# FFN start: second unit's fifth and sixth product ahead of the first unit's seventh, and GpSimd's sums for them released earlier

## The reference

```python
    u2 = _rmsnorm(h, ln2_g[i])
    a, bb = jnp.split(u2 @ w_gate_upffn[i], 2, axis=-1)
    h = h + (jax.nn.silu(a) * bb) @ w_down[i]
```

## Time and profile before

| what | value |
|---|---|
| time of the program, median of 3 | 1633.21 us (1632.21 to 1633.38) |
| time of the profiled execution | 1631.67 us |
| its span | 1629.7 us |
| TensorE busy (matmul) | 1605.5 us, 99% |
| VectorE busy | 1148.1 us, 70% |
| first product of unit 0 / of unit 2 starts | 458.06 / 499.22 us |
| VectorE busy in the 22.2 us from 457.80 to 480.00 | 22.13 us |
| VectorE busy in the 20 us from 480 to 500 | 19.16 us |
| TensorE busy in the 100 us from 600 to 700 | 100.00 us |

### The profile page before, as it was taken

One profiled execution on the slowest core, in us unless ns is written; L12 is line 12 of the kernel. 1 busy time (PEld: TensorE's weight loads), 2 busy tenths in 40 slices (PEclk: granted clock), 3 DMA queues, 4 the chain that ended last, 5 costly groups with the idle time before them and its releaser, 6 DMA issues.

```text
span 1629.7 us, 21081 instructions
## 1 busy us (share of the span) xinstructions
PE 1605.5 (99%) x7644; PEld 1307.3 (80%) x7644; DVE 1148.1 (70%) x1650; ACT 629.0 (39%) x1012; POOL 709.5 (44%) x390
## 2 busy tenths in 40 slices
PE   9999999999999999999999999999999999999997
PEld 5888888888877888888888788887878888877775
DVE  6342788863499777777776766886986995399557
ACT  6221444421165444444444222254562012268214
POOL 2435111155514333322226688671555554544552
PEclk9999999999999999999999999999999999999999
DMA  5511110141514443334449995323201111110012
GB/s 199 87 56 39 40 38 28 33 152 61 219 73 157 158 150 148 143 146 165 154 158 353 404 393 232 143 78 116 65 27 39 50 41 52 39 53 27 14 39 104
DMA packets 54566, 190.31 MB, mean 117 GB/s; under 512 B 5857, under 2 KB 7842, under 8 KB 53834
## 3 DMA queue, kind: packets, MB, share of 16 engines
q1 hardware_dynamic: 49362, 171.66, 29.0%
q10 hardware_dynamic: 5112, 17.44, 3.6%
HBM read 134.02 MB, written 55.05 MB: 116 GB/s over the span
## 4 chain that ended last, share of the span: by engine, by line
PE 84%; DVE 8%; issue 3%; DMA 2%; ACT 2%; POOL 1%; SPq 0%; DVEq 0%; ACTq 0%; POOLq 0%
PE G L832 37%; PE U L1102 11%; PE G L1102 10%; PE U L1140 6%; PE G L1140 6%; PE G L1176 4%; PE U L996 1%; DMA hid_spill<-hst 1%; PE U L1384 1%; DMA raw<-in_weights 1%; PE G L1373 1%; DVE ring_lo L2424 1%; DVE X_lo L2419 1%; DVE h L2529 1%; PE U L877 1%
## 5 line engine op out<-in xcount | busy, mean ns | idle before, releaser
L633 POOL TENSOR_SCALAR w_hi<-raw 128x1024 fp32r<-128x1024 f32 x48 | 143.0, 2979 | 274.0 <-PE G L832 213.4
L832 PE MATMUL G<-B_hi,w_hi 128*128 128x512 f32 x480 | 149.5, 393 | 0.2 <-ACT yb L1942 0.2
L832 PE MATMUL G<-B_lo,w_hi 128*128 128x512 f32 x480 | 148.0, 390 | 0.0
L832 PE MATMUL G<-B_hi,w_lo 128*128 128x512 f32 x480 | 147.9, 389 | 0.0
L832 PE MATMUL G<-A_hi,w_hi 128*128 128x512 f32 x432 | 138.4, 402 | 0.0
L677 POOL TENSOR_TENSOR S<-fraw 128x512 f32<-128x512 f32 x33 | 46.9, 1422 | 202.7 <-DVE ring_lo L2424 194.5
L832 PE MATMUL G<-A_lo,w_hi 128*128 128x512 f32 x432 | 133.6, 390 | 0.0
L832 PE MATMUL G<-A_hi,w_lo 128*128 128x512 f32 x432 | 133.3, 390 | 0.0
L635 POOL TENSOR_TENSOR w_lo<-raw,w_hi 128x1024 fp32r<-128x1024 f32 x48 | 127.6, 2658 | 4.0
L1667 ACT ACTIVATE ring_hi<-S 128x512 fp32r<-128x512 f32 x132 | 82.0, 628 | 111.8 <-PE U L1140 34.0
L1102 PE MATMUL G<-X_hi,ring_hi 128*128 128x512 f32 x308 | 120.1, 390 | 2.3 <-DVE sf L2439 1.2
(11 more groups left out here) (440 smaller groups left out, 3815.9 us busy)
## 6 DMA issues: line engine op xcount, KB each, us to landing
raw<-in_weights SPq DMA_DIRECT2D x72, 512.0 KB, 3.6
hid_spill<-hst SPq DMA_DIRECT2D x72, 512.0 KB, 2.6
fraw<-in_weights SPq DMA_DIRECT2D x66, 512.0 KB, 4.5
Dc<-hid_spill SPq DMA_DIRECT2D x56, 512.0 KB, 12.7
Dc<-hid_spill ACTq DMA_DIRECT2D x14, 512.0 KB, 7.9
h<-in_x_t SPq DMA_DIRECT2D x8, 512.0 KB, 7.8
h_spill<-h SPq DMA_DIRECT2D x8, 512.0 KB, 6.8
pj_spill<-pj_out SPq DMA_DIRECT2D x8, 512.0 KB, 3.6
```

What stands on the lines that cost most here:

```text
L633: pool.tensor_scalar(hi, raw[:, u, :], 1.0, None, ALU.mult).then_inc(w_hi_done, 1)
L832: mm = pe.matmul(G[g][:, b * HT:(b + 1) * HT], w, x[:, k, b * HT:(b + 1) * HT], start=s0, stop=s1)
```

## The change

Three things are changed, all in units 0 and 1 of the FFN. TensorE takes a new list `START` for its first 14 products, in which (1, 4) and (1, 5) stand ahead of (0, 6). The two special waits of GpSimd's sums for unit 1 are gone: S2 now waits for `weights_lo(0, 4)` and S4 for `weights_lo(0, 5)`, as in all other units. ScalarE's and VectorE's written orders are turned accordingly: on ScalarE `take(0, 4)` moves behind `weights_hi(1, 4)`, and `weights_hi(1, 6)` behind `weights_hi(2, 1)`. On VectorE `quarter(0, 1)` moves ahead of `operand_lo(5)`, then come `weights_lo(1, 4)`, `quarter(0, 3)`, `weights_lo(1, 5)`, and only then `weights_lo(0, 6)` and `operand_lo(6)`. The last pair of units keeps the old list.

```diff
+START = [(0, 0), (0, 1), (1, 0), (1, 1), (0, 2), (0, 3), (1, 2), (1, 3), (0, 4), (0, 5), (1, 4), (1, 5), (0, 6), (1, 6)]
 FIRST = [(0, 0), (0, 1), (1, 0), (1, 1), (0, 2), (0, 3), (1, 2), (1, 3), (0, 4), (0, 5), (0, 6), (1, 4), (1, 5), (1, 6)]
...
                 def free(r):
 
-                    if w == 1 and r == 5:
-                        pool.wait_ge(x_lo, 2 * NR)
-                    elif w == 1 and r == 4:
-                        pool.wait_ge(f_lo[0], turn(0, NR - 1))
-                    elif w:
+                    if w:
                         pool.wait_ge(f_lo[(w - 1) % 2], turn(w - 1, r))
...
-            for w, r in FIRST:
+            for w, r in START:
                 product(w, r)
...
-            take(0, 2), take(0, 4), take(1, 0), take(1, 2)
-            weights_hi(1, 4), weights_hi(1, 5), weights_hi(1, 6)
-            weights_hi(2, 0), weights_hi(2, 1)
+            take(0, 2), take(1, 0), take(1, 2)
+            weights_hi(1, 4), take(0, 4), weights_hi(1, 5)
+            weights_hi(2, 0), weights_hi(2, 1), weights_hi(1, 6)
             take(1, 4), silu(0)
...
-            weights_lo(0, 5), operand_lo(5)
-            weights_lo(0, 6), quarter(0, 1), quarter(0, 3), operand_lo(6)
-            weights_lo(1, 4), quarter(1, 1), quarter(1, 3), quarter(0, 4), weights_lo(1, 5)
-            quarter(0, 5), weights_lo(1, 6), quarter(0, 6), weights_lo(2, 0), weights_lo(2, 1)
+            weights_lo(0, 5), quarter(0, 1), operand_lo(5)
+            weights_lo(1, 4), quarter(0, 3), weights_lo(1, 5), weights_lo(0, 6), operand_lo(6)
+            quarter(0, 4), quarter(1, 1), quarter(1, 3), quarter(0, 5)
+            weights_lo(1, 6), quarter(0, 6), weights_lo(2, 0), weights_lo(2, 1)
             quarter(1, 4), weights_lo(2, 2), weights_lo(2, 3), gated_quarter(1, 1), gated_quarter(1, 4)
```

## The result

The changed kernel is slower: 1636.48 us median (1634.37 to 1638.92, 13 runs) against 1632.33 us for the kernel before (1630.94 to 1633.38, 11 runs), timed beside it. The ratio is 1.0025, 95% interval 1.0017 to 1.0032. The difference of the medians is 4.15 us; 4.1 was forecast. The profiled execution took 1634.37 us, the fastest of the 13 runs.

A forecast was written before the change was run, and what follows sets the result against it. TensorE is busy 1605.5 of 1629.7 us, and the time of `quarter(0,6)` was taken to set (2,6). Adding 3.5 + 0.55 = 4.1 us to the 1633.21 median gave 1637.3, range 1634.0 to 1639.0 (8 in 10).

The forecast's parts named there:

- Part 3: (0,6) directly ahead of (1,6) in ring slot 6: refill exposed, TensorE waits 1.6 us, `quarter(0,6)` 3.5 us later.
- Part 2: New order up to (1,4): after `operand_lo(5)` and `weights_lo(1,4)`, product (1,4) starts at 489.0.
- Part 1: Unit 1's freed GpSimd sums collide with VectorE at `operand_lo(4)`, 1.10 us, and `operand_lo(5)`, 0.8: 1.9 us.
- the prediction's own sign: On VectorE: the prediction is wrong if VectorE isn't held up near 480.6 and 485.2.
- The last term: At `weights_lo(1,6)`: a collision with GpSimd's unit 2 sums costs 0 to 1.10 us, half taken, 0.55.
- the sum 3.5 + 0.55: `quarter(0,6)` 3.5 us later plus 0.55 for a collision at `weights_lo(1,6)`: 4.1 us in all.
- The reading of what carries everything: The time of `quarter(0,6)` sets the start of (2,6), by a fixed chain of 21.65 us.
- (B): GpSimd's freed sums don't hold VectorE up, 1.9 us not paid: +1.6 to +2.7, no measurable change; chance 0.24.
- (C): Full block at `weights_lo(1,6)` and one more between 500 and 520: +5.7 us, 1638.9; chance 0.12.
- (D): (1,4) follows (0,5) at once, short refill at (1,6), up to 1.87 us back: 1631.3; chance 0.07.
- No new wait behind: After (2,6), expected near 521 in place of 516.87, no new wait was to appear.
- Part 4's spare time: On ScalarE: `weights_hi(1,6)` behind `weights_hi(2,0)` and `(2,1)`, whose load lands by 495.65, has 0.6 us to spare.

The follow-up runs named there:

- e3: Changed kernel with (0,6) between (1,4) and (1,5), ScalarE's and VectorE's orders turned to fit; ratio to before 1.0011, `operand_lo(4)` to unit 3 40.93 us.
- e5: Kernel before with only GpSimd's two special waits removed, no order touched; ratio to before 1.0000, `operand_lo(4)` to unit 3 39.14 us.
- e8: Changed kernel with `quarter(0,3)` directly behind `quarter(0,1)`, ahead of `operand_lo(5)`; one run, `operand_lo(4)` to unit 3 43.15 us against 42.86.
- e2: Changed kernel with unit 1's S2 and S4 over 8 of 512 columns, the rest left out; ratio to before 1.0010, `operand_lo(4)` to unit 3 41.13 us.
- e4: Kernel before with `quarter(0,6)` ahead of `weights_lo(1,6)` on VectorE; timed three times, ratios to before 0.9994, 0.9993 and 0.9994.
- e1: Changed kernel with `quarter(0,6)` ahead of `weights_lo(1,6)` on VectorE; ratio to before 1.0020, `operand_lo(4)` to unit 3 41.92 us.
- e7: Changed kernel with the edits of e2 and e3 at once; ratio to before 1.0000, `operand_lo(4)` to unit 3 39.13 us.
- e9: Rebuilt kernel: TensorE's and ScalarE's orders as in e3, VectorE's quarters and refills reordered; ratio to before 1.0000, `operand_lo(4)` to unit 3 39.29 us.
- e6: Changed kernel with `weights_lo(0,4)` ahead of `weights_lo(1,3)` on VectorE; one run, `operand_lo(4)` to unit 3 42.78 us against 42.86.

## Why the prediction was right

**The side, the size and most of the path were right.** Slower by over 0.2% was forecast with 0.62; the ratio is 1.0025 with the lower end of its interval, 1.0017, just under that bound, so slower is clear of the interval and over 0.2% only likely. The median, 1636.48, lies 0.8 below the forecast and in the range. That 0.8 comes from the starting point, a median of three runs (1633.21) that lay 0.9 above the 1632.33 of the eleven; the difference itself is 4.15 where 4.1 was forecast, closer than the interval (2.8 to 5.2 us) can tell.

**Part 3, the slot, was right.** Forecast: (0,6) over at 497.3, (1,6) at 498.9 plus up to 1.1, a new wait of 1.6 to 2.7. Measured: 497.01, 498.97, and 1.80. e3 takes 1.93 of the 3.66 away by putting one product between the two users.

**Part 2 was right**: (1,4) was forecast at 489.0 and came at 488.71.

**Part 1 came out near in its sum and wrong in its step.** The step "GpSimd then gets its turn, and `operand_lo(4)` waits 1.10" failed: GpSimd was kept out for 4.9 us and `operand_lo(4)` was not touched. By the prediction's own sign, VectorE held up near 480.6 and 485.2, half of it failed: there was no delay at 480.6, and no wait of (0,4) for `X_lo`. Both sums then fell on `operand_lo(5)`, 1.59 in place of the 1.9 reckoned for the two places. That the sum nearly held is luck in part, since e5 shows the same freed sums costing nothing where quarters happen to lie right, and e8 S4 kept out altogether. That collisions of this kind are on the path is shown by e2: 1.73, with the smaller one at `weights_lo(1,6)` in it.

**The last term was 0.37, not 0.55**: `weights_lo(1,6)` lasted 1.05 in place of 0.68. In the prediction's terms the sum 3.5 + 0.55 came out as 3.25 + 0.37 = 3.62 at `quarter(0,6)`, the 3.25 being smaller by the 0.3 that Part 1 had reckoned too much.

**The reading of what carries everything held for the change, and was stated too strongly.** From `quarter(0,6)` to (2,6) it is 21.65 before, 21.66 in the changed kernel, and 21.69 in e4. But it is 22.36 in e1, 22.61 in e7, 22.84 in e3 and 23.42 in e9. The chain isn't fixed: it is the longest of several of nearly one length, and where the quarter is pulled ahead in a new product order, ScalarE's queue (e3, e7, e9) or VectorE's with its collisions with unit 2's sums (e1, e9) takes over. It foretells what a delay costs better than what an advance brings.

**Rivals.** (B), no collision on the path, is refuted by e2; its remark that GpSimd might be let in later did come true, but the sums then fell on `operand_lo(5)` and were paid all the same. (C), two more full blocks, didn't come. (D), all hidden, didn't come: (1,4) did follow (0,5) at once, but (0,5) had itself waited 1.49, and the refill ahead of (1,6) was not short.

**No new wait behind** was forecast; there is one of 0.45 ahead of (2,5), which costs nothing at (2,6).

**Part 4's spare time** for `weights_hi(1,6)` behind unit 2's tiles was put at 0.6; it was 0.17, and e8 shows what happens when it is gone.

**What stays open.** Unit 3 starts 3.66 late, but the span is only 2.7 longer. TensorE's timelines of the down products, the first matmul of all, in the changed kernel and before, and the only one with a wait in the next 20 us, before:

```profile
885.76 0.61 PE L1137 MATMUL G<-Dc,ring_hi 128*128 128x512 f32 x2
```

```profile
882.15 0.62 PE L1140 MATMUL G<-Dc,ring_hi 128*128 128x512 f32 x2
...
901.99 0.70 PE L1140 MATMUL G<-Dc,ring_hi 128*128 128x512 f32 x2 [0.64 <-DVE h L2529]
```

Up to the start of the down products the delay is carried almost whole: 3.61. Most of what is given back is the wait of 0.64 at 901.99 for VectorE's `h`, which the trace of the changed kernel doesn't have. This wait takes one of three sizes in the 14 traces: none (changed, e5, e6), about 0.6 (before and seven others, the three of e4's kernel among them), and 1.8 (e1, e7, e9). So one pair of spans is a poor measure of the change. The medians, 4.15 apart, don't show the 0.8 given back. Whether the size of this wait belongs to a kernel or to an execution was not tested.

## What to carry to other kernels

When two products share a ring slot, the gap between them must cover the way TensorE, ScalarE, VectorE and back: here 1.96 us from the end of (0,6) to the start of (1,6), and it also delays whatever stands behind the refill in those two queues. Before freeing an engine that shares a port with a saturated one, look at which instructions it will fall on: what counted here was whether a window of its own length, in which the other engine has an input in PSUM or pauses, lay there, and not how early it might start. And of two ready instructions in a saturated queue, the one that a longer chain hangs on goes first; swapping `quarter(0,6)` with `weights_lo(1,6)` was worth more here (1.03) than any new product order that was tried (nothing).

## What the runs showed of the hardware

GpSimd and VectorE do not simply take turns. In the kernel before they did at 462.6. But in the changed kernel GpSimd, whose S2 starts at 478.60 while `turn_x(3)` is at work, let both halves of `operand_lo(4)` and `weights_lo(0,5)` pass in front of it, though each began after it, and in e5 it waited out some 8 us. In every such case it got in when VectorE had an instruction with an input in PSUM, or a pause (e8, 487.69). The Trainium skill, page "SBUF — State Buffer", section "Who interferes with whom", says that the shared pair of ports is an exclusive lock and that issue order decides who blocks. The rows here agree with the lock: the first half of `operand_lo(5)` had to wait for the rest of S2. They do not agree with the order, going by the starts of the rows: S2 was there at 478.60, and `operand_lo(4)`, which starts at 480.64, went first. An instruction of 8 columns that needs 0.20 us can so last 5.06 (e2).

Between the halves of `operand_lo(5)` S4 did get in, in the changed kernel but not in e8; one difference is that in the changed kernel VectorE itself had just been blocked. That can't be all, for at 462.6 VectorE had not been blocked. Another difference lies in the sums: the one that got its turn at 462.6 was an S1, which reads two loaded tiles, and so was the one in e9 (start 501.47, 1.61 us long) that got in ahead of VectorE's row of 501.85; those kept out are all S2 or S4, which read another sum. Which of these decides, if any, was not tested; e6 rules out the width of the instruction that is at work.
